# RWKV projections of a four-layer step: the second low-rank weights in another buffer, the second mix and the key and bonus sums at other places

## Chip, cores and metric

One core of a Trainium2 chip runs the whole program. The metric is the device time of one execution in microseconds (us), the median of several executions.

## The reference

A sequence of 320 tokens (64 decoded, 256 of a prompt) with 1024 features goes through four layers. Each has a mixer and a convolutional feed-forward block. Layers 0 and 3 have sparse attention, layer 2 latent attention, and layer 1 an RWKV-7 mixer. The change lies in layer 1:

```python
xm = h[:, :, None, :] + xx[:, :, None, :] * mu
xr, xw, xk, xv, xa, xg = [xm[:, :, i] for i in range(6)]
r = xr @ w_rkv[0]
k = xk @ w_rkv[1]
v = xv @ w_rkv[2]
w_log = -jax.nn.softplus(-(w0 + jnp.tanh(xw @ w1) @ w2)) - 0.5
a = jax.nn.sigmoid(a0 + (xa @ a1) @ a2)
g = jax.nn.sigmoid(xg @ g1) @ g2
kk = kk / jnp.maximum(jnp.sqrt(jnp.sum(kk * kk, axis=-1, keepdims=True)), 1e-12)
k = k * (1 + (a - 1) * k_a)
...
bonus = jnp.sum(hs(r) * hs(k) * r_k, axis=-1, keepdims=True) * hs(v)
```

`h` is the normed input, `xx` the difference to the token before. A "mix" is one of the `xm`. `kk` is normed for each head of 64 features. A recurrence in chunks of 64 tokens follows the projections.

## The kernel before, in words

Activations lie transposed: 1024 features are 8 tiles of 128 partitions, with 320 tokens in the free dimension. Every fp32 product is made of three: ScalarE rounds the weights of a slab to their high part (`split_hi`, L1731), VectorE subtracts for the low part (`split_lo`, L2276), and TensorE multiplies high by high, high by low and low by high (L950 to L952). Raw, high and low weights have two buffers each, slab n in buffer n % 2, and SP loads the raw weights (L554). The split of slab n on ScalarE waits for TensorE's end with slab n-2, and TensorE's start with slab n for VectorE's split of it.

The projections of layer 1 (`pe_rwkv`, L1290) are 24 output tiles in 12 slabs: tiles 0 to 7 are k, 8 to 15 r, 16 to 23 v. A tile is 24 matmuls into bank i % 2. The engines run lists that are written out by hand; semaphores alone hold them together. Slabs are counted from the start of the stage here: tile i belongs to slab i // 2.

Inputs of the three projections are three mixes (`mix(j, first, end)`, L2542). VectorE computes a tile of the mix into one of two buffers xn (L2530), ScalarE rounds it to the high part (`high`, L2010) and VectorE subtracts (L2547). The first and third mix use XH and XL, the second XH2 and XL2.

The low-rank part has a first product (L1296) with L1 and L1X and three middle activations (`middle`). The second product (`lora_rows`, TensorE L1324, ScalarE L2022) uses the weights L2. It has eight rows m of three matmuls. TensorE does rows 2i and 2i+1 behind tile i, for i of 0 to 3, in two sets of banks; ScalarE evacuates them to LW, A and G.

Behind other tiles TensorE does small products with a constant: `key_sums` (L1332, sums of squares for each head), `key_fans` (L1339, the inverse norms spread out again) and `bonus_sums` (L1345). Fan m (m of 2 or more) waits on TensorE until VectorE has used fan m-2 in `key_heads(m-2)` (L2595). VectorE starts key head 0 only behind the third mix, the scans of the decays (`decays`, L2582) and the splits of slabs 6 and 7. The key heads are in two groups, 0 to 4 and 5 to 7, with the split of slab 8 between them. `inverse(g)` (L2567) waits for ScalarE's `key_roots(g)` (L2041). `keys_and_rows(m)` (L2629) and `bonus(m)` (L2612) follow on VectorE, while POOL multiplies the keys (L738 to L745), each m held by ScalarE's `key_gain(m)` (L2045). ScalarE's tile i copy is L2033.

The buffers of layer 1 stand one behind the other from `over`, each of [128, 8, 320] fp32: HN, XX, LW, R, K, A, VV, then one more (`over_s`) with L1X and XL2 on it, then G, with L1 on it. XH2 lies on VV. R is written from tile 8 on, VV from tile 16 on.

Of the kernel before, what the change touches and what calls it, by code (L numbers as in the profile page):

```python
# [14 lines left out]
F32 = mybir.dt.float32  # L15
# [5 lines left out]
D, KD = 1024, 8  # L21
SEQ, DEC, PAST = 256, 64, 128
T = DEC + SEQ
# [135 lines left out]
def build(nc, i_, o_):  # L159
# [61 lines left out]
    with ExitStack() as ctx:  # L221
        base = [-(-nc.sbuf_base // 64) * 64]

        def at(name, shape, dt, offset):
            return nc.alloc_sbuf_tensor_at(name, shape, dt, offset=offset)

        def size(shape):
            b = 4
            for x in shape[1:]:
                b *= x  # L230
            return -(-b // 64) * 64
# [33 lines left out]
        over = base[0]  # L265
# [16 lines left out]
        def vcol(name, j):  # L282
            return V[:, VOFF[name] + j:VOFF[name] + j + 1]
# [70 lines left out]
        over_s = over + 7 * size([128, KD, T])  # L354
# [8 lines left out]
        TK = at("TK", [128, 2, T], F32, rms_at)  # L363
        L1 = at("L1", [128, KD, 256], F32, over_s + size([128, KD, T]))
        L1X = at("L1X", [128, KD, 128], F32, over_s)
        L2 = at("L2", [128, 2, D], F32, over_s - size([128, KD, T]))
        XH2 = at("XH2", [128, KD, T], F32R, over_s - size([128, KD, T]))
        XL2 = at("XL2", [128, KD, T], F32R, over_s)

# [172 lines left out]
        def _(sp):  # L542
# [25 lines left out]
            def low_rank_weights():  # L568

                sp.wait_ge(x_done, 8 * xs_of[norm_of[1, "mix"]] + 8)  # L570
                for dst, src in ((L2[0:64, 0, :], i_["b_w2"][0]), (L2[64:128, 0, :], i_["b_a2"][0]), (L2[:, 1, :], i_["b_g2"][0])):
                    sp.dma_start(dst, src).then_inc(lora_in, 16)
# [358 lines left out]
        def _(pe):  # L931
# [358 lines left out]
            def pe_rwkv(layer):  # L1290
# [24 lines left out]
                def lora_rows(m):  # L1315
# [6 lines left out]
                    for a in range(3):  # L1322
                        r_ = (slice(0, 64), slice(64, 128), slice(0, 128))[a]
                        pe.matmul(psum[(2, 5)[m % 2] + a][:, 0:T], L2[r_, int(a == 2), 128 * m:128 * m + 128], (LTg if a == 2 else LT)[r_, :],  # L1324
                                  start=True, stop=True).then_inc(lora_out, 1)
# [19 lines left out]
                    pe.matmul(psum[6 + m % 2][:, 0:T], C("headsum"), xn[:, m % 2, :], start=True, stop=True).then_inc(hs_done, 1)  # L1345

                sums_at = {5: (0, 1), 6: (2, 3), 7: (4, 5), 8: (6, 7)}
                fans_at = {12: (0, 1), 13: (2, 3, 4), 14: (5, 6, 7)}
                bonus_at = {18: (0,), 19: (1,), 20: (2,), 22: (3, 4), 23: (5, 6, 7)}
                for i in range(24):  # L1350
                    n, j = s0 + i // 2, i // 8
                    ready(n)
# [360 lines left out]
            for layer in range(DEPTH):  # L1713
                (dsa, pe_rwkv, pe_mla)[layer % 3](layer)
                ffn(layer)

        @block.scalar
        def _(act):
            chain = Chain(act, act_c)

            def split_hi(n, n_expr=None, raw_count=None):

                s_ = slabs[n]
                act.wait_ge(w_raw[n % 2], raw_after[n] if raw_count is None else raw_count)
                if n_expr is None:
                    if n >= 2:
                        act.wait_ge(mm_done, done_after[n - 2])
                else:
                    act.wait_ge(mm_done, n_expr)
                w_ = s_.kt * s_.w  # L1730
                act.activation(hi[n % 2][:, 0:w_], raw[n % 2][:, 0:w_], ACT.Copy).then_inc(w_hi, 1)  # L1731
# [271 lines left out]
            def act_rwkv(layer):  # L2003
# [4 lines left out]
                def high(j, k):  # L2008
                    act.wait_ge(mix_raw, KD * j + k + 1)
                    act.copy((XH, XH2, XH)[j][:, k, :], xn[:, k % 2, :]).then_inc(mix_hi, 1)  # L2010

                def highs(j, first, end):
                    for k in range(first, end):
                        high(j, k)
# [7 lines left out]
                def lora_rows(m):  # L2022
                    for a in range(3):
                        act.wait_ge(lora_out, 3 * m + a + 1)
                        ps = psum[(2, 5)[m % 2] + a][:, 0:T]
                        if a < 2:
                            act.activation((LW, A)[a][:, m, :], ps, ACT.Sigmoid, bias=vcol(("b_w0", "b_a0")[a], m)).then_inc(lora_evac, 1)
                        else:
                            act.copy(G[:, m, :], ps).then_inc(lora_evac, 1)

                def tile(i):
                    act.wait_ge(mm_done, done + i + 1)
                    act.copy((K, R, VV)[i // 8][:, i % 8, :], psum[i % 2][:, 0:T]).then_inc(rkv_evac, 1)  # L2033

                def key_squares(m):
                    if m >= 2:
                        act.wait_ge(hs_done, m - 1)
                    act.wait_ge(rkv_evac, m + 1)
                    act.activation(sq[:, m % 2, :], K[:, m, :], ACT.Square, scale=vcol("b_k_k", m)).then_inc(kk_sq, 1)
# [21 lines left out]
                for i in range(4):  # L2061
                    tile(i)
                    if i % 2:
                        split_hi(s0 + i // 2 + 2)
                    lora_rows(2 * i)
                    lora_rows(2 * i + 1)
                highs(1, 0, 4)
                tile(4)
                key_squares(0)
                key_squares(1)  # L2070
                highs(1, 4, 8)
                tile(5)
                key_squares(2)
                key_squares(3)
# [188 lines left out]
            for layer in range(DEPTH):  # L2263
                (dsa, act_rwkv, act_mla)[layer % 3](layer)
                ffn(layer)

        @block.vector
        def _(dve):
            chain = Chain(dve, dve_c)

            def split_lo(n, count=None):

                s_ = slabs[n]
                dve.wait_ge(w_hi, n + 1 if count is None else count)
                w_ = s_.kt * s_.w
                dve.tensor_tensor(lo[n % 2][:, 0:w_], raw[n % 2][:, 0:w_], hi[n % 2][:, 0:w_].bitcast(F32),  # L2276
                                  ALU.subtract).then_inc(w_lo, 1)
# [235 lines left out]
            def dve_rwkv(layer):  # L2513
# [15 lines left out]
                def mixed(dst, k, mu):  # L2529
                    return dve.scalar_tensor_tensor(out=dst, in0=XX[:, k, :], scalar=vcol("b_mu", 8 * mu + k),  # L2530
                                                    in1=HN[:, k, :], op0=ALU.mult, op1=ALU.add)
# [10 lines left out]
                def mix(j, first, end):  # L2542
                    lows = (XL, XL2, XL)[j]

                    def low(k):
                        dve.wait_ge(mix_hi, KD * j + k + 1)
                        dve.tensor_tensor(lows[:, k, :], xn[:, k % 2, :], (XH, XH2, XH)[j][:, k, :].bitcast(F32), ALU.subtract  # L2547
                                          ).then_inc(mix_done, 1)

                    for k in range(first, end):  # L2550
                        if KD * j + k >= 2:
                            dve.wait_ge(mix_done, KD * j + k - 1)
                        mixed(xn[:, k % 2, :], k, (2, 0, 3)[j]).then_inc(mix_raw, 1)
                        if k > first:
                            low(k - 1)
                    low(end - 1)

                mix(0, 0, 8)
                split_lo(s0 + 1)
                split_lo(s0 + 2)  # L2560
                dve.wait_ge(lora_out, 24)
                mix(1, 0, 4)
                split_lo(s0 + 3)
                mix(1, 4, 8)
                split_lo(s0 + 4)

                def inverse(g):  # L2567
# [270 lines left out]
            for layer in range(DEPTH):  # L2838
                (dsa, dve_rwkv, dve_mla)[layer % 3](layer)
                ffn(layer)  # L2840
# [60 lines left out]
```

## Time and profile before

| what | value |
|---|---|
| median of 3 runs | 1671.02 us (1670.92 to 1672.31) |
| the profiled execution, span from first to last instruction | 1671.1 us |
| TensorE busy | 1597.7 us, 96% of the span |
| VectorE busy | 1136.3 us, 68% |
| ScalarE busy | 848.2 us, 51% |
| POOL busy | 722.7 us, 43% |
| mean granted clock of TensorE | 0.991 |
| tile 0 of the stage starts | 405.9 us |
| first products of the recurrence (L1385) | 531.5 us |

The profiled execution's own time is its span here; no other figure of it is given. Times within it are counted from its first instruction. PE is TensorE, PEld its weight loads, DVE VectorE, ACT ScalarE. Matmuls overlap, so that a matmul of 0.31 us is followed by the next after 0.15.

### The profile page before, as it was taken

What the parts mean: (1) busy time and instruction counts of PE and PEld (TensorE: products, weight loads), DVE (VectorE), ACT (ScalarE), POOL (GpSimd) and SP (SyncE); (2) the same over time, 40 slices, a digit from 0 to 9 for tenths busy, and PEclk for the clock granted to TensorE, in tenths of its full rate; (3) what the DMA queues carried; (4) which work ended last, traced back from release to release, by engine and by line L of the source; (5) the groups of instructions that cost most, each with busy time, mean ns of one, the idle gap of its engine ahead of it and who ended that gap; (6) DMA issues with size and microseconds to landing.
All of it is one profiled execution on the core that took longest, in us unless ns stands there. A gap on an engine that the chain in (4) does not pass through costs nothing.

```text
span 1671.1 us, 36269 instructions
## 1 busy us (share of the span) xinstructions
PE 1597.7 (96%) x13605; PEld 1521.9 (91%) x13605; DVE 1136.3 (68%) x2010; ACT 848.2 (51%) x1589; POOL 722.7 (43%) x778
## 2 busy tenths in 40 slices
PE   5989999998988999999999998999999999999998
PEld 5869999995788999999999877999999878999997
DVE  4877777636487566677764766777764797777743
ACT  4465665434653433455643475555643455655633
POOL 6754666200046211466621451466621764566600
PEclk9999999999999999999999999999999999999999
DMA  7324556453230003555545421555545512555453
GB/s 234 92 71 128 151 151 168 124 152 94 96 108 26 10 4 109 145 147 147 139 135 170 144 81 52 140 147 147 141 135 164 162 53 84 157 146 147 133 145 104
DMA packets 331755, 203.94 MB, mean 122 GB/s; under 512 B 7753, under 2 KB 327385, under 8 KB 331521
## 3 DMA queue, kind: packets, MB, share of 16 engines
q1 hardware_dynamic: 329136, 195.45, 40.6%
q0 software_dynamic: 1776, 5.60, 1.0%
q8 instruction: 74, 1.21, 0.3%
q10 hardware_dynamic: 736, 1.41, 0.2%
q14 instruction: 33, 0.26, 0.1%
HBM read 198.95 MB, written 3.39 MB: 121 GB/s over the span
## 4 chain that ended last, share of the span: by engine, by line
PE 79%; DVE 8%; ACT 4%; POOL 4%; issue 4%; DMA 0%; SPq 0%; DVEq 0%; POOLq 0%; ACTq 0%
PE bank L950 22%; PE bank L951 22%; PE bank L952 22%; PE bank L1385 4%; DVE lo L2276 2%; ACT hi L1731 2%; POOL lo L664 1%; PE bank L962 1%; PE bank L1599 1%; PE bank L1296 1%; DVE SC L2465 1%; POOL ssq L653 1%; POOL qsin L684 1%; PE bank L1004 1%; PE bank L1324 1%
## 5 line engine op out<-in xcount | busy, mean ns | idle before, releaser
L950 PE MATMUL bank<-XH,hi 128*128 128x320 f32 (+1 forms) x1912 | 601.2, 314 | 16.3 <-DVE lo L2306 9.0
L2276 DVE TENSOR_TENSOR lo<-raw,hi 128x2048 fp32r<-128x2048 f32 (+2 forms) x195 | 416.4, 2136 | 276.7 <-ACT hi L1731 276.7
L951 PE MATMUL bank<-XL,hi 128*128 128x320 f32 (+1 forms) x1912 | 592.6, 310 | 0.0
L952 PE MATMUL bank<-XH,lo 128*128 128x320 f32 (+1 forms) x1912 | 592.5, 310 | 0.0
L1731 ACT ACTIVATE hi<-raw 128x2048 fp32r<-128x2048 f32 (+2 forms) x203 | 355.7, 1752 | 70.6 <-PE bank L952 64.0
L950 PEld LDWEIGHTS bank<-XH,hi 128*128 128x128 f32 (+1 forms) x1912 | 360.6, 189 | 28.0 <-DVE lo L2306 9.0
L951 PEld LDWEIGHTS bank<-XL,hi 128*128 128x128 f32 (+1 forms) x1912 | 360.6, 189 | 1.3
L952 PEld LDWEIGHTS bank<-XH,lo 128*128 128x128 f32 (+1 forms) x1912 | 360.4, 189 | 0.0
L711 POOL TENSOR_TENSOR upad<-upad,rstd 128x128 f32<-128x128 f32 (+1 forms) x176 | 167.7, 973 | 199.7 <-ACT upad L1839 199.7
L950 PE MATMUL bank<-GH,hi 128*128 128x322 f32 x704 | 220.1, 313 | 1.8 <-DVE lo L2276 1.8
L951 PE MATMUL bank<-GL,hi 128*128 128x322 f32 x704 | 218.7, 311 | 0.0
L952 PE MATMUL bank<-GH,lo 128*128 128x322 f32 x704 | 218.0, 310 | 0.0
L716 POOL COPY ust<-upad 128x4 f32 (+1 forms) x176 | 210.8, 1228 | 13.5 <-POOL upad L711 13.0
L653 POOL TENSOR_TENSOR ssq<-ssq,sq 128x320 f32<-128x320 f32 x66 | 75.4, 1142 | 284.3 <-ACT sq L1887 223.8
L2393 DVE SCALAR_TENSOR_TENSOR conv<-upad,V,conv 128x322 f32<-128x322 f32 x352 | 171.0, 548 | 0.0
L1838 ACT COPY upad<-bank 128x64 f32<-128x64 f32 x176 | 39.2, 223 | 233.2 <-PE bank L952 233.2
L950 PEld LDWEIGHTS bank<-GH,hi 128*128 128x128 f32 x704 | 132.7, 188 | 2.5 <-DVE lo L2276 2.3
L951 PEld LDWEIGHTS bank<-GL,hi 128*128 128x128 f32 x704 | 133.1, 189 | 0.0
L952 PEld LDWEIGHTS bank<-GH,lo 128*128 128x128 f32 x704 | 132.4, 188 | 0.0
L1849 ACT ACTIVATE conv<-upad,V 128x322 f32<-128x322 f32 x176 | 106.2, 652 | 7.4 <-POOL upad L711 4.1
L1887 ACT ACTIVATE sq<-xT 128x320 f32<-128x320 f32 (+1 forms) x32 | 15.1, 472 | 132.9 <-DVE xT L2417 132.9
L1839 ACT COPY upad<-bank 128x256 f32<-128x256 f32 x176 | 68.0, 393 | 0.0
(388 smaller groups left out, 2265.3 us busy)
## 6 DMA issues: line engine op xcount, KB each, us to landing
raw<-in_f_w_up SPq DMA_DIRECT2D x176, 512.0 KB, 5.0
raw<-in_f_w_down SPq DMA_DIRECT2D x64, 704.0 KB, 4.6
raw<-in_a_w_in SPq DMA_DIRECT2D x13, 1024.0 KB, 5.5
raw<-in_b_w_rkv SPq DMA_DIRECT2D x12, 1024.0 KB, 5.2
raw<-in_a_w_out SPq DMA_DIRECT2D x8, 1024.0 KB, 5.2
raw<-in_b_w_out SPq DMA_DIRECT2D x4, 1024.0 KB, 5.5
raw<-in_c_w_out SPq DMA_DIRECT2D x4, 1024.0 KB, 5.2
raw<-in_c_w_uq SPq DMA_DIRECT2D x3, 1024.0 KB, 5.1
```

The source lines that it names most:

```text
L653: pool.tensor_tensor(ssq[:, :], ssq[:, :], sq[:, (c - 1) % 2, :], ALU.add).then_inc(ssq_done, 1)
L711: ins = pool.tensor_tensor(upad[:, j, :, cols_], upad[:, j, :, cols_], rstd[:, c:c + n_].rearrange("p (o n) -> p o n", o=1).to_broadcast([ ...
L716: ins = pool.tensor_copy(ust[:, seg, :, :].rearrange("p r (h f) -> p h r f", h=2)[:, :, :, bass.ds(f, 1)].rearrange("p h r f -> p h (r f)" ...
L950: pe.matmul(out, a, xh(k), start=(start and k == 0), stop=False)
L951: pe.matmul(out, a, xl(k), start=False, stop=False)
L952: last = pe.matmul(out, b, xh(k), start=False, stop=(stop and k == kt - 1))
L1385: last = pe.matmul(out[r_, col(q)], lhs(e, r_, q), rhs(e, r_, q), start=opens and (closes or q == 0), stop=closes, skip_group_check=True)
L1731: act.activation(hi[n % 2][:, 0:w_], raw[n % 2][:, 0:w_], ACT.Copy).then_inc(w_hi, 1)
L1839: ins = act.copy(upad[:, j, h, 68:TG + 2], ps[h][:, 64:T])
L1849: ins = act.activation(conv[:, j, h, :], upad[:, j, h, 2:TG + 2], ACT.Identity, scale=V[:, bass.ds(f + (w_ + NF * h), 1)], bias=V[:, bass. ...
L2276: dve.tensor_tensor(lo[n % 2][:, 0:w_], raw[n % 2][:, 0:w_], hi[n % 2][:, 0:w_].bitcast(F32), ALU.subtract).then_inc(w_lo, 1)
L2393: dve.scalar_tensor_tensor(out=conv[:, j, h, :], in0=upad[:, j, h, tap:tap + TG], scalar=V[:, bass.ds(f + (w_ + NF * h), 1)], in1=conv[:, ...
```

## The change

L2 moves from the place of VV to the place of R. On TensorE the key fans move up one tile each, and the bonus sums are dealt out anew. On ScalarE two casts of the second mix stand between the low-rank rows 2i and 2i+1, instead of two groups of four behind tile 3 and the first squares. On VectorE the second mix no longer waits for the last low-rank product, but for the first middle product (`lora_mid`), and stands around the splits of slabs 2 and 3 in pairs of two tiles.

```diff
-        L2 = at("L2", [128, 2, D], F32, over_s - size([128, KD, T]))
+        L2 = at("L2", [128, 2, D], F32, over + 3 * size([128, KD, T]))
...
                 sums_at = {5: (0, 1), 6: (2, 3), 7: (4, 5), 8: (6, 7)}
-                fans_at = {12: (0, 1), 13: (2, 3, 4), 14: (5, 6, 7)}
-                bonus_at = {18: (0,), 19: (1,), 20: (2,), 22: (3, 4), 23: (5, 6, 7)}
+                fans_at = {11: (0, 1), 12: (2, 3, 4), 13: (5, 6, 7)}
+                bonus_at = {18: (0,), 19: (1,), 20: (2,), 21: (3,), 22: (4, 5), 23: (6, 7)}
...
                     if i % 2:
                         split_hi(s0 + i // 2 + 2)
                     lora_rows(2 * i)
+                    highs(1, 2 * i, 2 * i + 2)
                     lora_rows(2 * i + 1)
-                highs(1, 0, 4)
                 tile(4)
                 key_squares(0)
                 key_squares(1)
-                highs(1, 4, 8)
                 tile(5)
...
                 mix(0, 0, 8)
                 split_lo(s0 + 1)
+                dve.wait_ge(lora_mid, 1)
+                mix(1, 0, 2)
+                mix(1, 2, 4)
                 split_lo(s0 + 2)
-                dve.wait_ge(lora_out, 24)
-                mix(1, 0, 4)
+                mix(1, 4, 6)
+                mix(1, 6, 8)
                 split_lo(s0 + 3)
-                mix(1, 4, 8)
                 split_lo(s0 + 4)
```

## Rows read from the trace of the kernel before

**Rows 1.** The page, parts 1 and 4: busy time, and the chain by engine.
```profile
PE 1597.7 (96%) x13605; PEld 1521.9 (91%) x13605; DVE 1136.3 (68%) x2010; ACT 848.2 (51%) x1589; POOL 722.7 (43%) x778
PE 79%; DVE 8%; ACT 4%; POOL 4%; issue 4%; DMA 0%; SPq 0%; DVEq 0%; POOLq 0%; ACTq 0%
```

**Rows 2.** Busy time by stretch: PE, PEld, DVE, ACT, POOL, then clock, DMA share, GB/s.
```profile
405.00:436.00 31.00, 28.37 (x148) 19.66 (x148) 11.04 (x16) 17.93 (x36) 1.02 (x2) 1.00 0.22 68
```

**Rows 3.** VectorE in order of time, 422 to 456 us: start, duration, line, [idle before, releaser].
```profile
422.88 2.29 DVE L2276 TENSOR_TENSOR lo<-raw,hi 128x2048 fp32r<-128x2048 f32 x1 [7.33 <-ACT hi L1731]
436.51 1.01 DVE L2530 SCALAR_TENSOR_TENSOR xn<-XX,V,HN 128x320 f32<-128x320 f32 x2 [11.33 <-PE bank L1324]
...
443.70 1.01 DVE L2530 SCALAR_TENSOR_TENSOR xn<-XX,V,HN 128x320 f32<-128x320 f32 x2
...
446.76 1.10 DVE L2547 TENSOR_TENSOR XL<-xn,XH 128x320 fp32r<-128x320 f32 x2
...
453.39 0.33 DVE L2569 TENSOR_SCALAR TK<-TK 128x320 f32<-128x320 f32 x1 [0.68 <-ACT TK L2043]
...
455.82 0.92 DVE L2530 SCALAR_TENSOR_TENSOR xn<-XX,V,HN 128x320 f32<-128x320 f32 x2
```

**Rows 4.** ScalarE in order of time, 448 to 453 us.
```profile
448.48 1.90 ACT L1731 ACTIVATE hi<-raw 128x2048 fp32r<-128x2048 f32 x1
...
451.62 1.28 ACT L2043 ACT_TABLE_LOAD   x1
```

**Rows 5.** TensorE's matmuls in order of time, 448 to 495 us.
```profile
448.18 1.18 PE L1332 MATMUL bank<-sq,con 128*32 128x320 f32 x4 [0.29 <-ACT sq L2039]
...
463.56 0.42 PE L950 MATMUL bank<-XH,hi 128*128 128x320 f32 x1 [1.74 <-DVE lo L2276]
...
472.18 0.41 PE L950 MATMUL bank<-XH,hi 128*128 128x320 f32 x1 [0.58 <-DVE lo L2276]
...
476.63 0.41 PE L950 MATMUL bank<-XH,hi 128*128 128x320 f32 x1
...
480.87 1.23 PE L1339 MATMUL bank<-TK,con 32*128 32x320 f32 x4 [0.46 <-DVE AR L2595]
...
483.08 0.41 PE L950 MATMUL bank<-XH,hi 128*128 128x320 f32 x1
...
488.34 0.81 PE L1339 MATMUL bank<-TK,con 32*128 32x320 f32 x4
...
490.57 0.41 PE L950 MATMUL bank<-XH,hi 128*128 128x320 f32 x1
...
494.19 0.31 PE L950 MATMUL bank<-XH,hi 128*128 128x320 f32 x1
```

**Rows 6.** VectorE in order of time, 469 to 524 us.
```profile
469.86 2.27 DVE L2276 TENSOR_TENSOR lo<-raw,hi 128x2048 fp32r<-128x2048 f32 x1
...
478.00 2.27 DVE L2276 TENSOR_TENSOR lo<-raw,hi 128x2048 fp32r<-128x2048 f32 x1
480.19 1.00 DVE L2595 SCALAR_TENSOR_TENSOR AR<-K,V,bank 128x320 f32<-128x320 f32 x2
...
496.66 2.56 DVE L2276 TENSOR_TENSOR lo<-raw,hi 128x2048 fp32r<-128x2048 f32 x1 [1.29 <-ACT hi L1731]
499.15 1.17 DVE L2600 TENSOR_TENSOR A<-AR,A 128x320 f32<-128x320 f32 x1
...
523.04 0.48 DVE L2600 TENSOR_TENSOR A<-AR,A 128x320 f32<-128x320 f32 x1
```

**Rows 7.** Busy time by stretch of 4 us, as in rows 2: two stretches of low clock.
```profile
388.00:392.00 4.00, 1.30 (x3) 0.94 (x4) 3.93 (x6) 2.86 (x2) 0.00 (x0) 0.54 0.92 285
...
484.00:488.00 4.00, 4.00 (x19) 4.00 (x18) 1.60 (x1) 2.92 (x4) 3.92 (x4) 0.59 0.20 66
```

**Rows 8.** ScalarE's gain 4 and POOL's first product with it, in order of time.
```profile
496.52 0.65 ACT L2048 ACTIVATE sq<-A,onemka,V 128x320 f32<-128x320 f32 x1
...
499.93 1.13 POOL L738 TENSOR_TENSOR A<-A,XX 128x320 f32<-128x320 f32 x1
```

## The prediction

> **What bounds the kernel now.** The page's busy shares and the shares of the chain that ended last come first: TensorE is busy 96% of the span and carries 79% of the chain [rows 1]. So the kernel is bound by TensorE, and a change counts only where TensorE waits. The change touches one stage, the 24 tiles of the RWKV projections, 405.9 to about 530 us. I then read the queues of TensorE, VectorE and ScalarE in order of time through that stage.
>
> In the first part (tiles 0 to 3 with the low-rank rows) TensorE never waits for long, while VectorE is busy 11.0 of 31 us and ScalarE 17.9 [rows 2]. VectorE stands idle twice there: 7.33 us before the split of slab 2, and 11.33 us before the second mix, which waits until the last low-rank row is through TensorE [rows 3]. From 436.5 on VectorE has that mix, the splits, the third mix, the scans and the key heads one behind the other, and TensorE waits for it: 1.74 us ahead of tile 10, 0.58 ahead of tile 12, and at the key fans, which wait for the key heads [rows 5]. In this stage VectorE sets the pace.
>
> **The change part by part.**
>
> *L2 under R in place of VV.* The three loads keep their number, their size and their place on SP's queue, and nothing behind them moves. R is first written by tile 8, far behind the last low-rank row. Cost 0 by itself. It lets XH2, which lies over VV, be written early; XL2, over L1X, needs the middle products alone, hence the new wait, which is met before VectorE gets there.
>
> *The second mix goes into the low-rank rows.* Half of it (4 tiles) runs from 443.70 to 447.86 [rows 3], 4.2 us, so 8.3 us of VectorE leave the stretch behind 436.5. In their new place the work has 7.33 and 11.33 us of holes. ScalarE's 8 casts of about 0.4 us go into 13.1 idle us (31 less 17.9) [rows 2]. Behind the casts on ScalarE stand the odd low-rank rows; TensorE asks for their banks only after one more tile of 3.5 us (476.63 to the fan behind tile 13, and 490.57 to 494.19 with its gap, show that length [rows 5]), so they stay covered. VectorE's split of slab 2 moves from 422.9 to about 425.5, since the casts of tiles 2 and 3 come behind ScalarE's split; TensorE wants it at 436.1. If that cover of 8 us were gone, it would cost the excess. I take 0 for all of this, within 0 to 0.5.
>
> *How much of the 8.3 us arrives.* The splits of slabs 3 and 4 come early. The next item, the inverse of the key norms, waits for ScalarE's root. That root needs the sums behind tile 6, which TensorE can hardly begin earlier: before, they started at 448.18 after a wait of 0.29 us [rows 5], so tile 6 is through at about 447.7 in both kernels. ScalarE then has a tile copy, two squares, the table load of 1.28 and the root, which brings it to 450.9. Before, the split of slab 4 was on ScalarE only at 448.48, behind the casts of the second mix, and the table load at 451.62 [rows 4], so the inverse came at 453.39 [rows 3]. The gain is 2.4 us, not 8.3; the other 5.9 go into a wait on VectorE. Bounds: 0 (a tile copy or a square in the way) and 3.5 (the third mix, begun at 455.82, can't go ahead of tile 7's end, which is two sums and 3.5 us later, 452.3). From there VectorE's list is the same and without long holes, so the split of slab 6 ends at 469.7 instead of 472.1 and the first key head starts at 477.8 instead of 480.19 [rows 6]. TensorE's tile 12 starts at 469.8 instead of 472.18 [rows 5] and ends at 473.4.
>
> *The key fans, one tile earlier.* Fans 0 and 1 behind tile 11 wait for the first inverse alone and are free. Fans 2, 3 and 4 now stand behind tile 12. Fan 2 waits for the first key head, and VectorE starts that only behind all scans and the split of slab 7. That is 477.8, so TensorE stands from 473.4 to about 478.3, with tile 13 queued behind the fans. Before, from the first head (480.19) to the tile behind fan 4 (483.08) it took 2.9 us [rows 5, 6]. So tile 13 starts at 480.7, against 476.63: **4.1 us late**, with 7.3 us behind tile 12 in which TensorE does three short fans. What is queued behind tile 13 is a second hole: fan 7, now ahead of tile 14, needs head 5, which needs VectorE's split of slab 8, which needs ScalarE's, which needs the weight buffer that tile 13 frees. From the end of tile 15 (494.19) to the end of VectorE's split of slab 9 (496.66 and 2.56) it is 5.0 us; without POOL beside it 4.8 [rows 5, 6]. With head 5 (0.5) and fan 7 to the tile (0.7 and a start of 0.1) the hole is 6.1 us. At full clock: tile 13 ends at 484.2, tile 14 runs 490.3 to 493.9, tile 15 starts at 493.9 against 490.57 [rows 5]: **3.3 us late**.
>
> *The clock.* Tile 14 took from 483.08 to 488.34, 5.26 us instead of 3.53 [rows 5], because the granted clock was 0.59 there, that is mostly the lower of its two levels, 1.2 GHz [rows 7]. Ahead of it TensorE had done three short fans in 3 us. After the layer's boundary it was 0.54 too, where TensorE had been idle for most of the stretch [rows 7]. In this kernel the drop of tile 14 is hidden, since fan 7 waited for VectorE until 489.9. In the new one nothing hides it: ScalarE's split waits for tile 13, and tile 14 has nothing to wait for. Both new holes (7.3 us with three fans, 6.1 with two) are longer than the 3 us that cost the clock in this trace. Price of one: 5.26 less 3.53, 1.73 us; bounds 0 (the 1.74 us ahead of tile 10 cost no clock) and 2.9 (a whole tile at 1.2 GHz takes 6.4). I take the price twice, since both holes are nearer to the rows with a drop. The Trainium skill (TensorE: Matmul & The Clock Gate, "HAM oscillation") says that every wait that is long enough sends the engine back to half rate and that this is paid again each time. By that rule both holes pay; by the row ahead of tile 10 alone neither would. That is the pair of cases below.
> Tile 15 then starts at 493.9 + 3.5 = 497.4, **6.8 us late**.
>
> *What is given back behind it.* The splits of slabs 9 and 10 follow TensorE and stay 6.8 late; behind slab 10's, VectorE has work without a break to the end of the stage. POOL's key products slow it: a product of 0.48 us takes 1.17 beside them [rows 6], a round of key decay and bonus row 3.4 instead of 1.5. Before, POOL took up pair 4 at 499.93, 2.8 us behind its gain's end (496.52 and 0.65) [rows 8], so it had a backlog. Now the gain is 6.8 late and the backlog is gone, POOL is only 4.0 late, and ends 2.8 us earlier by VectorE's count: 2.8/3.4 of a round less, times 1.9, is 1.6 us. Bounds 0 and 3.8 (two rounds).
>
> *The bonus sums.* Sum 3 one tile earlier, 4 and 5 behind tile 22, 6 and 7 behind 23. TensorE waits for the same last bonus row, which VectorE sets; the move costs 0, or takes up to 0.5 us off the end, because fewer sums are left behind tile 23.
>
> **Sum.** 3.3 + 2 x 1.73 - 1.6 = +5.2 us at the first products of the recurrence. From there on everything hangs on those products and moves as one. The profiled execution took 1671.1 us of span, 0.1 above the median of 1671.0. Median of after: 1676.2.
>
> **The rivals.**
> - *The clock holds in both holes.* For it: 1.74 us of wait at tile 10 left the clock at 1.00. Against: 3 us with fans did not. +3.3 - 1.6 = +1.7: 1672.7. Chance 0.10. This is the result of the row at tile 10 against the rule of the page.
> - *One of the two holes costs the clock.* +3.4: 1674.4, on the edge. Chance 0.17.
> - *The fans don't wait (the other side).* It is one mechanism: VectorE reaches the first key head by the end of tile 12. It decides at 473.4, which needs 6.8 us of advance where I find 2.4; for it speaks that 8.3 us were taken out of that queue, against it that tile 6 and tile 7 hold the root and the third mix. With the fans free TensorE keeps the advance, 2.4 us, and up to 3.5: 1668.6 to 1667.5. Chance 0.08.
> - *The move doesn't take place:* the casts hold up the low-rank rows, or VectorE is as late at the inverse as before. Then the first head is at 480.2, tile 13 a further 2.4 late: +7.6, 1678.6. Chance 0.05.
> - *Both holes cost the clock,* my forecast: 1676.2, its own range 1674.3 to 1678.4 (give-back 3.8 or 0, price of a drop 1.4 to 2.2). Chance 0.60.
>
> **How the numbers follow.** 0.2% of 1671 is 3.3 us, about what a measurement of this kernel can tell from no change. Slower by more than that: the forecast nearly whole (0.58), half of the one-hole case (0.08), the last rival: 0.70. Faster by more than 3.3 needs the whole 3.5: 0.03. The rest, 0.27, is within. The range takes in both clock cases, 1672.0, and goes to the upper bound of the forecast, 1678.5; the case of the other side is left out.
>
> **What would show it.** In the profile of after: the second mix's rows on VectorE between 415 and 439; the inverse near 451; TensorE's largest wait of the stage, 4 to 5 us, on a key fan (L1339) for VectorE's key head; a second one of about 4 us on a fan; a granted clock near 0.5 in tiles 13 and 14; tile 15 starting 5 to 7 us later than before, and less of that left at the recurrence's first products. The forecast is wrong if the fans show no long wait, if tile 13 starts ahead of 476.6, or if the rest of the kernel moves otherwise than the stage does.

## The result, and the profile after

The changed kernel took 1684.01 us (median, 1682.29 to 1687.28), the kernel before beside it 1671.66 us (1669.32 to 1676.04). The ratio is 1.0071, with a 95% interval of 1.0060 to 1.0083: slower by 0.71%, 11.9 us on 1671.7. The forecast was 1676.2, with a range of 1672.0 to 1678.5. The direction was right, and so were the two long waits; the size forecast, 5.2 us, was less than half.

The profiled execution of the changed kernel has a span of 1684.2 us. Tile 0 starts at 408.06 us there, against 405.92 before. That is not the change's doing, since it starts at 406.33 in a second profile of the same kernel, so times of two profiles are compared from tile 0 or from tile 4. The forecast's places, from tile 0, in us:

| from tile 0 | before | forecast | after |
|---|---|---|---|
| inverse of the key norms | 47.5 | 45.0 | 45.5 |
| first key head | 74.3 | 71.9 | 72.2 |
| tile 12 | 66.3 | 63.9 | 64.3 |
| tile 13 | 70.7 | 74.8 | 76.4 |
| tile 14 | 77.2 | 86.1 | 89.1 |
| tile 15 | 84.65 | 91.5 | 94.0 |
| first transposes of the recurrence | 124.6 | 129.8 | 135.0 |

VectorE in order of time, kernel after (start, duration, line, idle before it and releaser):

```profile
431.62 0.89 DVE L2546 TENSOR_TENSOR XL<-xn,XH 128x320 fp32r<-128x320 f32 x2 [1.05 <-ACT XH L2010]
...
439.49 0.89 DVE L2546 TENSOR_TENSOR XL<-xn,XH 128x320 fp32r<-128x320 f32 x2 [6.04 <-ACT XH L2010]
...
449.20 2.29 DVE L2275 TENSOR_TENSOR lo<-raw,hi 128x2048 fp32r<-128x2048 f32 x1 [6.62 <-ACT hi L1731]
453.53 0.33 DVE L2570 TENSOR_SCALAR TK<-TK 128x320 f32<-128x320 f32 x1 [2.03 <-ACT TK L2043]
...
455.96 0.92 DVE L2529 SCALAR_TENSOR_TENSOR xn<-XX,V,HN 128x320 f32<-128x320 f32 x2
...
480.30 1.00 DVE L2596 SCALAR_TENSOR_TENSOR AR<-K,V,bank 128x320 f32<-128x320 f32 x2
482.43 1.00 DVE L2596 SCALAR_TENSOR_TENSOR AR<-K,V,bank 128x320 f32<-128x320 f32 x2 [1.13 <-PE bank L1339]
...
492.93 2.29 DVE L2275 TENSOR_TENSOR lo<-raw,hi 128x2048 fp32r<-128x2048 f32 x1 [7.82 <-ACT hi L1731]
...
508.07 2.29 DVE L2275 TENSOR_TENSOR lo<-raw,hi 128x2048 fp32r<-128x2048 f32 x1 [8.03 <-ACT hi L1731]
```

The second mix is done at 440.4, 32.3 us from tile 0; before it took until 447.9, 41.9 from tile 0 [rows 3]. As forecast, most of the freed time turned into waits, 6.62 and 2.03 us, ahead of the split of slab 4 and the inverse. The first key head came at 72.2 from tile 0 instead of 74.3: 2.0 us earlier. The splits of slabs 8 and 9 then wait 7.82 and 8.03 us for ScalarE, and ScalarE waits for TensorE's tiles to free the weight buffers.

TensorE's waits in the stage, kernel after (engine, what waited, for what: sum, times, longest):

```profile
PE bank L1339 <- DVE AR L2596: 9.5, 3, 4.8
PE bank L1345 <- DVE xn L2610: 2.8, 2, 2.3
...
PE bank L950 <- DVE lo L2275: 0.5, 1, 0.5
```

And TensorE in order of time:

```profile
463.69 0.42 PE L950 MATMUL bank<-XH,hi 128*128 128x320 f32 x1 [0.53 <-DVE lo L2275]
...
472.40 0.41 PE L950 MATMUL bank<-XH,hi 128*128 128x320 f32 x1
...
480.99 1.86 PE L1339 MATMUL bank<-TK,con 32*128 32x320 f32 x4 [4.80 <-DVE AR L2596]
483.12 1.40 PE L1339 MATMUL bank<-TK,con 32*128 32x320 f32 x2 [0.27 <-DVE AR L2596]
484.45 0.64 PE L950 MATMUL bank<-XH,hi 128*128 128x320 f32 x1
...
490.56 0.81 PE L1339 MATMUL bank<-TK,con 32*128 32x320 f32 x4
...
495.83 1.40 PE L1339 MATMUL bank<-TK,con 32*128 32x320 f32 x2 [4.46 <-DVE AR L2596]
497.16 0.64 PE L950 MATMUL bank<-XH,hi 128*128 128x320 f32 x1
...
502.07 0.31 PE L950 MATMUL bank<-XH,hi 128*128 128x320 f32 x1
...
530.76 1.41 PE L1345 MATMUL bank<-xn,con 128*128 128x320 f32 x2 [2.27 <-DVE xn L2610]
531.50 0.94 PE L950 MATMUL bank<-XH,hi 128*128 128x320 f32 x1
...
536.48 1.24 PE L1345 MATMUL bank<-xn,con 128*128 128x320 f32 x4
```

The waits ahead of tiles 10 and 12 [rows 5] are down to 0.53 and nothing. In their place stand 4.80 us ahead of fan 2 and 4.46 ahead of fan 7, as forecast, and a third of 2.27 us ahead of bonus sum 3, behind tile 21, which was not. Tile 13 takes 6.11 us (484.45 to 490.56), tile 14 4.91, tile 22 4.98 (531.50 to 536.48) instead of 3.5. The step from the first key head to tile 13 takes 4.15 us (480.30 to 484.45); before it took 2.9.

The granted clock says why (stretch: PE, PEld, DVE, ACT, POOL, clock, DMA share, GB/s):

```profile
479.40:479.80 0.40, 0.00 (x0) 0.00 (x0) 0.40 (x1) 0.40 (x1) 0.00 (x0) 0.69 0.00 0
...
479.00:490.00 11.00, 8.74 (x27) 7.00 (x28) 3.86 (x6) 5.32 (x5) 6.73 (x8) 0.53 0.29 95
490.00:497.00 7.00, 2.54 (x11) 1.16 (x9) 3.21 (x3) 2.77 (x3) 3.40 (x3) 0.73 0.04 12
497.00:505.00 8.00, 8.00 (x45) 7.84 (x45) 2.73 (x6) 0.98 (x2) 3.20 (x4) 0.81 0.35 123
526.00:532.00 6.00, 3.73 (x21) 3.10 (x20) 5.93 (x8) 0.79 (x2) 5.63 (x6) 0.90 0.00 0
532.00:538.00 6.00, 6.00 (x33) 5.68 (x32) 4.15 (x12) 1.09 (x3) 0.05 (x1) 0.82 0.13 44
```

Of two levels, a share of 0.53 over 11 us is 10.3 us at the lower one, and the five longer stretches add up to some 20 us of 1.2 GHz, against 3.3 us in the stretch of [rows 7] before. The first row shows where it begins: at about 479.5, 1.4 us before fan 2 can start.

### The profile page after: what moved, and what is told of

It is laid out like the page before. It is cut to its first block, busy times and chain, and to the rows that moved or that the text cites. A ratio compares the mean times of both kernels' runs of the same rounds, so it can differ in the third digit from the quotient of the medians.

```text
span 1684.2 us, 36269 instructions
## 1 busy us (share of the span) xinstructions
PE 1606.1 (95%) x13605; PEld 1529.9 (91%) x13605; DVE 1132.6 (67%) x2010; ACT 848.4 (50%) x1589; POOL 717.6 (43%) x778
## 4 chain that ended last, share of the span: by engine, by line
PE 80%; DVE 8%; ACT 4%; issue 4%; POOL 4%; DMA 1%; SPq 0%; DVEq 0%; POOLq 0%; ACTq 0%
PE bank L950 22%; PE bank L951 22%; PE bank L952 22%; PE bank L1385 4%; DVE lo L2275 2%; ACT hi L1731 2%; POOL lo L664 1%; PE bank L962 1%; PE bank L1296 1%; PE bank L1599 1%; PE bank L1324 1%; DVE SC L2464 1%; POOL ssq L653 1%; POOL qsin L684 1%; PE bank L1004 1%
```

## The experiments

Three accounts were to be told apart. **Theory 1:** the fans, one tile early, wait for VectorE, and each hole costs the clock as well. **Theory 2:** the moved mix or the place of L2 costs something. **Theory 3:** the bonus deal carries a large part. Whole medians turned out to be coarse: the kernel before itself gave medians of 1671.7 to 1676.0 in five comparisons, and single runs of 1669.3 to 1681.8. So each kernel is also judged by a stretch of its profile, from tile 4 to the recurrence's first transposes. (The expectations count from tile 0. In five of the profiles a stretch of low clock at tile 0 already added 0.9 to 1.3 us; tile 4 starts behind that, 30.15 us after tile 0 in the others.)

| kernel | tile 4 to recurrence, us | ratio, 95% interval |
|---|---|---|
| before | 94.5 | |
| after | 104.8 | 1.0071 (1.0060 to 1.0083) |
| after, again | 104.0 | 1.0050 (1.0037 to 1.0062) |
| before with the new fans | 106.0 | 1.0063 (1.0046 to 1.0081) |
| before with the new bonus deal | 94.2 | 0.9991 (0.9978 to 1.0004) |
| after, old fans | 93.1 | 0.9996 (0.9985 to 1.0007) |
| after, old bonus deal | 103.6 | 1.0054 (1.0039 to 1.0068) |
| after, both old | 94.6 | 0.9997 (0.9985 to 1.0009) |
| after, hole 1 filled | 102.0 | 1.0030 (1.0018 to 1.0041) |
| after, holes 1 and 2 filled | 99.2 | 1.0011 (0.9999 to 1.0024) |
| after, all three filled | 97.7 | 1.0009 (0.9995 to 1.0023) |
| after, fans spread later, old bonus | 93.4 | 1.0002 (0.9989 to 1.0016) |
| after, both old, lightly filled | 93.1 | 0.9982 (0.9971 to 0.9993) |
| before, lightly filled | 94.5 | 0.9986 (0.9974 to 0.9999) |

### Which part costs: one put back, one done alone

Old fans in the changed kernel:

```diff
-                fans_at = {11: (0, 1), 12: (2, 3, 4), 13: (5, 6, 7)}
+                fans_at = {12: (0, 1), 13: (2, 3, 4), 14: (5, 6, 7)}
```

> The changed kernel with the key fans back at tiles 12, 13 and 14. Theory 1 (fans 2 and 7, one tile earlier, hold TensorE, and the holes cost the clock): both long waits of 4.8 and 4.5 us on the fans go, tile 13 starts about 2 us earlier than in the kernel before (the 2.0 us that the first key head came forward, counted from tile 0), the low clock of 17 us in the stage shrinks to at most 3.4, and the time is 1668 to 1671. Theory 2 (the second mix among the low-rank rows, or L2 in its new place, costs something that the stage hides elsewhere): the time stays at 1678 or above. Theory 3 (the new deal of the bonus sums carries a large part, through its own wait of 2.3 us and the clock behind it): the wait on bonus sum 3 stays and the time is 1673 to 1676.

Measured: median 1673.71, before 1675.02, ratio 0.9996. Taken by itself, 1673.71 lies in the range of theory 3 and above that of theory 1; but the kernel before stood at 1675.02 beside it, not at 1671, so the ratio and the stretch have to decide. The long waits are gone, and the stretch is 11.7 us shorter than in the changed kernel and 1.4 shorter than before. Theory 2 falls. The wait of 1.88 us on bonus sum 3 stayed, as theory 3 had it, and the clock fell behind it (tile 22 took 5.3 us), but the loss was gone all the same. The gain expected by theory 1 (1668 to 1671) didn't show in the whole time.

Old bonus deal in the changed kernel:

```diff
-                bonus_at = {18: (0,), 19: (1,), 20: (2,), 21: (3,), 22: (4, 5), 23: (6, 7)}
+                bonus_at = {18: (0,), 19: (1,), 20: (2,), 22: (3, 4), 23: (5, 6, 7)}
```

> The changed kernel with the bonus sums dealt out as before. Theory 1: the fans carry the loss, so the time falls only by what the third hole cost: the wait of 2.27 us ahead of tile 22 goes, and with it the low clock in tile 22 (4.98 us instead of 3.5), less what the sums wait for later; 1.5 to 3 us under the changed kernel, 1681 to 1682.5. Theory 3 (the bonus deal carries a large part): 1677 or below. If the old deal only moves the same wait to the end, the time stays at 1684.

Measured: median 1683.89, ratio 1.0054. That is not the 1681 to 1682.5 expected, but the time named for a wait that only moves to the end; and the sums did wait 2.6 us in all at the end, after 2.8 in the changed kernel. The clock held in tile 22 (3.5 us). The stretch is 1.2 us shorter than in the first profile of the changed kernel and 0.4 shorter than in the second, so the deal's own price isn't shown here. It is small at most, and theory 3 falls as the main cause.

The new fans alone in the kernel before:

```diff
-                fans_at = {12: (0, 1), 13: (2, 3, 4), 14: (5, 6, 7)}
+                fans_at = {11: (0, 1), 12: (2, 3, 4), 13: (5, 6, 7)}
```

> The kernel before with the key fans alone one tile earlier; L2, the second mix and the bonus sums as before. Theory 1: the first key head comes at 480.2 there too, so fan 2 waits 5 us or more behind tile 12 (which starts at 472.2 and ends at 475.7, so about 4.7), the second hole is the same, and the time is that of the changed kernel plus the 2 us that the moved mix gains: 1684 to 1687. Theory 2 (the mix and L2 cost): under 1676.

Measured: median 1685.87 (four runs), ratio 1.0063, within what theory 1 expected. This one line is enough for the whole loss. TensorE's waits there are the same three on the fans:

```profile
PE bank L1339 <- DVE AR L2595: 9.5, 3, 4.8
```

The new bonus deal alone in the kernel before:

```diff
-                bonus_at = {18: (0,), 19: (1,), 20: (2,), 22: (3, 4), 23: (5, 6, 7)}
+                bonus_at = {18: (0,), 19: (1,), 20: (2,), 21: (3,), 22: (4, 5), 23: (6, 7)}
```

> The kernel before with the bonus sums alone dealt out anew. If the deal costs as in the changed kernel, the sum ahead of tile 22 waits about 1.9 us for VectorE, the sums behind tile 23 save less than that, and the stretch from tile 0 to the recurrence is 125.2 to 126.2 us instead of 124.6; the median moves by less than can be measured. If it costs nothing (as forecast), 124.6 or less.

Measured: median 1673.09, ratio 0.9991, stretch from tile 0 124.3 us. The sum ahead of tile 22 did wait 1.9 us, but the clock held (tile 22 took 3.8 us), and the end came no later. The expected cost wasn't there: in this profile the deal is free, as forecast.

Both old in the changed kernel (the two diffs at the head of this section together):

> The changed kernel with fans and bonus sums both as before: what is left of the change is the move of L2 and of the second mix. Theory 1: the first key head and everything behind it come 2.0 us earlier than before, counted from tile 0, and no wait is longer than before: ratio 0.998 to 0.999 against the kernel before. If the new bonus deal is itself a cost (its wait of 1.9 us and a stretch of low clock stood in the profile of the run with the fans alone put back), this one is 1 to 2 us faster than that; if the bonus sums only wait elsewhere, both are equal. Rival: the move gains nothing (ratio 1.000), because what comes forward on VectorE is lost at the end of the stage.

Measured: median 1673.56, ratio 0.9997. The first key head came 2.0 us earlier, yet the stretch is 94.6 us, that of the kernel before. The rival was right about the result, not about the place. The gain was lost in the clock. The profile of this run:

```profile
480.00:488.00 8.00, 6.45 (x34) 4.69 (x34) 4.34 (x6) 6.77 (x8) 7.16 (x7) 1.00 0.43 133
488.00:496.00 8.00, 7.25 (x25) 6.42 (x26) 5.61 (x9) 0.65 (x1) 7.84 (x9) 0.57 0.42 131
```

The low clock of tile 14 [rows 7] came later, behind the wait for fan 7, and fell on tile 15, which took 6.1 us (82.67 to 88.78 from tile 0). Before, it was hidden under the wait for fan 7; here nothing covers it. That is this profile, not a rule: with the fans alone put back, the lists are the same up to tile 20, and there the low clock fell on tile 14, under the wait for fan 7, and tile 15 took 3.6 us. So where the low stretch falls differs from profile to profile, and the whole times of both kernels (0.9997 and 0.9996) show no gain.

The changed kernel once more:

> The changed kernel once more, beside the others of this call. The stretch from tile 0 to the recurrence is again 134 to 136 us with 17 to 21 us of low clock in it, and the median is 1682 to 1686, or 10 us over the kernel before; if the first profile was an unlucky one, the stretch is 131 or less.

Measured: median 1683.24, ratio 1.0050, 135.4 us from tile 0 and 104.0 from tile 4. The waits are the same (4.8, 4.5 and 2.3 us), tile 13 took 5.6 us and tile 14 6.25, so the first profile was no exception for the two long holes. The third is another matter: sum 3 waited the same 2.27 us, and the clock held, so that tile 22 took 3.8 us and not 5.0:

```profile
526.00:532.00 6.00, 3.73 (x25) 3.34 (x24) 5.93 (x8) 0.60 (x3) 5.62 (x6) 1.00 0.00 0
532.00:538.00 6.00, 5.94 (x37) 5.30 (x37) 5.70 (x16) 1.39 (x3) 0.35 (x1) 1.00 0.13 44
```

### The clock by itself: holes filled, waits kept

Idle matmuls, whose results nobody reads, stand where TensorE waits anyway. No wait is taken away, and nothing of the computation is left out. Two holes filled:

```diff
+                FILL = {2: 30, 7: 28}
...
                     for m in fans_at.get(i, ()):
+                        if m in (2, 7):
+                            wf = tuple(parts(n + (m == 7)))[0]
+                            for z in range(FILL[m]):
+                                pe.matmul(psum[6][:, 0:T], wf[:, z % 8, 0:128], XH2[:, z % 8, :], start=True, stop=True)
                         key_fans(m)
```

> The changed kernel with 30 idle matmuls (full shape, into a free bank, read by nobody) ahead of fan 2 and 28 ahead of fan 7, where TensorE waits anyway; no wait is taken away. Theory 1 with the clock: the granted clock stays at 2.4 GHz through tiles 13 and 14, so these take 3.5 us each instead of 6.1 and 4.9, the steps from a key head to the tile behind its fans are back at 2.9 and 1.3 us, and the time falls by 4 to 6 us against the changed kernel, to 1678 to 1680. Rival (the tiles are long for another reason, or the clock follows something else than TensorE's work): tiles 13 and 14 stay at 6 and 5 us and the time stays at 1684 or rises by up to 0.5.

Measured: median 1676.32, ratio 1.0011, a lower time than the 1678 to 1680 expected. The stretch fell by 5.6 us (4.7 against the second profile), and the ratio by 0.6% (0.4% against the kernel's second measurement): 4 to 6 us had been expected. Tile 22 still took 5.3 us, behind the third hole.

Only the first (`FILL = {2: 30, 7: 0}`):

> The changed kernel with the idle matmuls ahead of fan 2 alone. Filling both holes took 8 us off. If each hole has its own price, tile 13 and its fans run at full clock (3.5 us instead of 6.1, and 1.3 us less for the steps of the fans), the hole ahead of fan 7 still costs the clock in tile 14 (4.9 to 5.3 us), and the time is half way, 1679 to 1681. If only the first one matters (the clock then holds over the second), 1676; if only the second, 1683 to 1684.

Measured: median 1679.40, ratio 1.0030, half way. Each hole has its own price: by the stretch 2.8 us for the first (104.8 to 102.0) and 2.8 for the second (102.0 to 99.2). The start of tile 15, which the third hole can't touch, says 2.7 for the first (3.4 against the second profile of the changed kernel) and 2.8 for the second.

All three, with the two fills above and this:

```diff
                     for m in bonus_at.get(i, ()):
+                        if m == 3:
+                            for z in range(14):
+                                pe.matmul(psum[4][:, 0:T], XH[:, z % 8, 0:128], XH[:, z % 8, :], start=True, stop=True)
                         bonus_sums(m)
```

> The changed kernel with idle matmuls ahead of fan 2 (30), fan 7 (28) and bonus sum 3 (14), so that TensorE is busy in all three holes of the stage. Filling two took the stretch from tile 0 to the recurrence's first transposes from 135.0 to about 130 us. Theory 1: the clock now stays up behind the third hole too (tile 22 takes 3.5 us instead of 5.0), and the stretch is 1 to 1.5 us shorter, 128 to 129; what is left against the 124.6 us of the kernel before is the price of the waits alone, 4 us. The median is 1674 to 1677. Rival: the end is set by VectorE alone and the stretch stays at 130.

Measured: median 1676.10, ratio 1.0009, 127.9 us from tile 0 and 97.7 from tile 4. The whole time can't tell this from two holes filled (1.0011); the stretch can, by 1.5 us. TensorE in order of time in this run (L1368 are the idle matmuls):

```profile
473.82 4.56 PE L1368 MATMUL bank<-XH,hi 128*128 128x320 f32 x30
478.80 1.23 PE L1339 MATMUL bank<-TK,con 32*128 32x320 f32 x4 [0.41 <-DVE AR L2604]
480.30 0.77 PE L1339 MATMUL bank<-TK,con 32*128 32x320 f32 x2 [0.27 <-DVE AR L2604]
481.00 0.41 PE L950 MATMUL bank<-XH,hi 128*128 128x320 f32 x1
...
484.71 0.81 PE L1339 MATMUL bank<-TK,con 32*128 32x320 f32 x4
485.45 4.38 PE L1368 MATMUL bank<-XH,hi 128*128 128x320 f32 x28
489.99 0.77 PE L1339 MATMUL bank<-TK,con 32*128 32x320 f32 x2 [0.16 <-DVE AR L2604]
490.69 0.41 PE L950 MATMUL bank<-XH,hi 128*128 128x320 f32 x1
```

and its granted clock by stretch:

```profile
472.00:480.00 8.00, 7.59 (x48) 6.71 (x46) 7.50 (x10) 5.03 (x5) 0.84 (x2) 1.00 0.39 129
480.00:488.00 8.00, 7.73 (x48) 6.66 (x48) 2.07 (x4) 4.95 (x5) 6.28 (x9) 1.00 0.34 118
488.00:496.00 8.00, 7.84 (x51) 7.17 (x50) 5.60 (x9) 0.98 (x2) 5.09 (x5) 1.00 0.40 131
516.00:524.00 8.00, 7.73 (x50) 7.17 (x49) 7.93 (x8) 1.85 (x5) 7.63 (x7) 1.00 0.00 0
524.00:532.00 8.00, 7.94 (x51) 7.30 (x50) 7.63 (x20) 1.38 (x3) 0.33 (x1) 1.00 0.12 35
```

Fans 2 and 7 still hold tiles 13 and 14 back until VectorE comes, but the clock is 1.00 throughout and tile 13 takes 3.7 us (481.00 to 484.71). So the loss of the stage parts in two: 7.1 us are the clock (104.8 less 97.7) and 3.2 the waits (97.7 less 94.5). With the second profile of the changed kernel (104.0) the clock's part is 6.2.

### Can the advance of 2 us be kept?

Fans later instead of earlier, old bonus deal:

```diff
-                fans_at = {11: (0, 1), 12: (2, 3, 4), 13: (5, 6, 7)}
+                fans_at = {12: (0, 1), 13: (2, 3), 14: (4, 5, 6), 15: (7,)}
```

> The moved mix with the fans later instead of earlier: 0 and 1 behind tile 12, 2 and 3 behind 13, 4 to 6 behind 14, 7 behind 15; bonus sums as before. Theory 1: each fan finds its key head done or nearly done, TensorE has no wait over 0.5 us on a fan and keeps its clock in tile 14. The stage ends 3 to 4 us earlier than in the kernel before, ratio 0.997 to 0.998, and 1 us under the run with fans and bonus as before. Rival: VectorE and POOL set the end of the stage, and the time equals that run's.

Measured: median 1674.06, ratio 1.0002. Tile 16 started at 84.5 from tile 0, 3.8 us ahead of the kernel before (88.3), but the stretch is 1.0 us shorter only: TensorE's waits on bonus sums were 3.6 us in this run (3.0 before), and the last thing that it waits for is VectorE. The ratio of 0.997 to 0.998 that theory 1 expected didn't come, and one wait on a fan was 0.72 us, not under 0.5. The rival comes nearer than theory 1.

Both old, and 3, 2 and 4 idle matmuls ahead of fans 2, 4 and 7:

```diff
                     for m in fans_at.get(i, ()):
+                        if m in (2, 4, 7):
+                            for z in range({2: 3, 4: 2, 7: 4}[m]):
+                                pe.matmul(psum[6][:, 0:T], XH2[:, z, 0:128], XH2[:, z, :], start=True, stop=True)
                         key_fans(m)
```

> The moved mix with fans and bonus sums as before, and 3, 2 and 4 idle matmuls ahead of fans 2, 4 and 7, about as much as TensorE waits there. Without them the 2 us that came forward were given back to a stretch of low clock in tiles 14 and 15. If the fill keeps the clock: stretch from tile 0 to the recurrence 122 to 123 us against 124.6 before, median 1 to 2 us under the kernel before. If so light a fill doesn't keep it: 124.5 to 125.5, and no gain.

Measured: median 1671.89 against 1674.07, ratio 0.9982 (0.9971 to 0.9993), the version whose interval stays furthest below 1. The clock held through tiles 14 and 15:

```profile
480.00:488.00 8.00, 7.37 (x40) 5.29 (x38) 4.33 (x7) 6.16 (x7) 7.79 (x7) 1.00 0.39 131
488.00:496.00 8.00, 7.88 (x51) 7.47 (x52) 6.64 (x8) 3.44 (x4) 7.84 (x9) 1.00 0.42 133
```

The stretch from tile 0 was 123.3 us, not 122 to 123: at the end, the sums waited 3.6 us for VectorE here too. The run with the fans alone put back, without a fill, has the same stretch from tile 4 (93.1) and a ratio of 0.9996, so this stage doesn't explain the difference in the whole time.

The same fill in the kernel before:

> The kernel before with the same 3, 2 and 4 idle matmuls ahead of fans 2, 4 and 7, the second mix and L2 where they were. It tells whether the gain of the moved mix with the light fill (stretch 123.3 us, ratio 0.9982) needs the moved mix. If it does: the low clock of tile 14 goes, but that was hidden by the wait of fan 7, so the stretch from tile 0 to the recurrence stays at 124.2 to 125 us and the ratio at 0.9995 to 1.0005. If the fill alone does it: 123.5 or less and 0.998 to 0.999.

Measured: ratio 0.9986 (0.9974 to 0.9999), stretch from tile 4 94.5 us as before. The stage says that the gain needs the moved mix, as expected; the whole time says that the fill alone may do nearly as well. The intervals overlap. What the fill gives to the whole time, and where, is left open.

## Why the prediction was right or wrong

**The second mix among the low-rank rows, at no cost:** right. From tile 4 back, tiles 0 to 4 take 30.1 us in both kernels, and the split of slab 2 was early enough.

**How much arrives (2.4 of 8.3 us):** right in kind, 2.0 us. The root is 0.5 us later than worked out; in part that is the squares behind tile 6, which waited 0.23 us for a sum. The table load began at 43.7 from tile 0 (451.76) against 45.7 before (451.62, [rows 4]).

**The fans, 4.1 us late at tile 13:** the mechanism was right, down to the wait (4.80 us; 4 to 5 forecast). Tile 13 was 5.7 us late. The 1.6 between are 0.3 from the smaller advance and 1.3 from fans that ran at the lower clock: VectorE's key heads waited 1.13 us for a fan instead of 0.50. The forecast priced the clock in the tiles and left out the fans ahead of them.

**The clock, 1.73 us a hole:** this is the step that failed. With both holes filled, tile 15 starts 58.3 us behind tile 4. In the changed kernel it is 63.9 and, again, 64.6, and 64.1 with the old bonus deal. So the clock cost 5.5 to 6.3 us at the two holes, 2.8 to 3.1 each, at and over the upper bound of 2.9. The price was read off tile 14 of the kernel before [rows 5, 7], where the clock fell when the tile had already run for 0.8 us, and came back after 3.4 us:

```profile
483.80:484.20 0.40, 0.40 (x4) 0.40 (x4) 0.00 (x0) 0.40 (x2) 0.40 (x2) 0.62 1.09 387
...
487.00:487.40 0.40, 0.40 (x4) 0.40 (x3) 0.40 (x1) 0.00 (x0) 0.40 (x1) 0.62 0.00 0
```

Behind the longer hole it was low before fan 2 was issued and for 10.3 us in all, so fans, tile and whatever waits for them all paid.

**Given back, 1.6 us, and the bonus deal at no cost:** wrong together. Tile 15 was 9.4 us late from tile 0, the recurrence 10.4, so 1.0 more was lost. The forecast had POOL end 2.8 us earlier by VectorE's count. It ended 7.4 us late, 2.0 ahead of tile 15's 9.4 and not 2.8. Its own gains stood behind tiles 14 and 15 on ScalarE, and it was idle for 4.80 us ahead of gain 3, which came at 502.59:

```profile
503.33 0.88 POOL L738 TENSOR_TENSOR A<-A,XX 128x320 f32<-128x320 f32 x1 [4.80 <-ACT sq L2048]
```

Yet with all three holes filled, only 0.5 us were given back (3.8 late at tile 15, 3.3 at the recurrence). Why the rest of it didn't reach the end isn't shown.

The other part is the third hole. Sum 3 behind tile 21 waited 2.3 us for VectorE in four profiles: in three of them the clock fell again in tile 22, and the recurrence came 40.9 to 41.0 us behind tile 15; in the fourth, the changed kernel's second, it held, and they were 39.4 us apart, as with the old deal or all holes filled. So the new deal costs 1.5 us where the clock falls behind it, and nothing where it doesn't. The forecast looked for a wait at its end and left out the clock.

Term by term for the stage, forecast and measured (the first profile): waits at tile 15 3.3 and 3.8, clock at the two holes 3.5 and 5.5, the third hole 0 and 1.5, given back 1.6 and 0.5. That makes 5.2 and, but for rounding, 10.4 us. With the price of the clock alone put right, the forecast would have been 7.2 to 8.0 us, still under what was measured; the miss took the other terms as well.

**The rest of the kernel moves as one:** not shown. The ratio gives 11.9 us and, in the second measurement, 8.4; the stretch 10.4 and 9.5. Behind the stage the same code took 1140.6 us before, 1141.2 after, and between 1137.4 and 1146.1 in the other profiles. What lies between 10.4 and 11.9 can't be placed.

**The chances and the range:** slower by more than 0.2% had 0.70. The forecast's own bounds, 2.9 us a hole and nothing given back, add up to 3.3 + 5.8 = 9.1, that is 1680.1. The range went to 1678.5, with a price of 1.4 to 2.2 for which no row stands; and the ends given for the case, 1674.3 and 1678.4, are not what its parts add up to (3.3 + 2.8 - 3.8 and 3.3 + 4.4, 1673.3 and 1678.7).

## What to carry to other kernels

A small product that waits for another engine, placed in TensorE's queue, holds back everything behind it; before it is moved up one place, the time at which its input is ready must be compared with the time at which its new place is reached, here 480.3 us (the first key head) against 476.2 (the end of tile 12) in the changed kernel. A hole in TensorE's queue can cost its length and then a stretch of half speed: here 7.1 of 10.4 us in one profile and 6.2 of 9.5 in the other. A stretch of low clock that sits under a wait is free as long as the wait covers it. And idle matmuls in the hole show how much of a loss is clock.

## What the runs showed of the hardware

The low clock was paid for again at both long holes, of 4.8 and 4.5 us, in every profile that has them unfilled. The Trainium skill (TensorE: Matmul & The Clock Gate, "HAM oscillation") has it that the change of clock is paid for anew at each such wait; the traces agree, with 5.5 to 6.3 us for the two in the three profiles that can be compared. Behind a third wait of 2.3 us the clock fell in three profiles, at about 1.5 us, and held at 1.00 in a fourth.

Four idle matmuls and fewer ahead of the fans went with a clock of 1.00 where 0.57 had stood without them, in the one profile that each has. Since the low clock comes at different places in kernels that are the same there, and the run with the later fans kept 1.00 in tiles 13 to 16 without any fill, that is not a proof.

At 1.2 GHz small products slow everything that waits for them: a key head's wait for its fan went from 0.50 to 1.13 us.

The same program's single runs spread over 1669.3 to 1681.8 us. In the profiles, stretches of low clock stand at different places in kernels that are the same there, for one at tile 0 in some and not in others. That sets the size of what whole times can tell here.
